# Fifth row tile of the early output projection: operand split before the barrier, products in the ramp behind it

## The reference

```python
h = rms_norm(x, g_attn); proj = h @ w_in          # 1376 columns for three groups of heads
out_a = sliding-window attention, 8 heads          # 512 columns
out_b = latent attention, 4 heads, chunk-causal    # 256 columns
out_m = cross-attention into 256 memory tokens     # 256 columns
x = x + concat(out_a, out_b, out_m) @ w_o          # 1024 x 1024
x = x + square(relu(rms_norm(x, g_ffn) @ w_ff1)) @ w_ff2
```

## Time and profile before

| what | value |
|---|---|
| time, median of 3 runs | 2163.74 us (2161.92 to 2166.23) |
| profiled execution, own time | 2162.71 us |
| its span | 2160.9 us |
| mean granted TensorE clock | 0.992 |
| busy, share of the span | PE 98%, PE weight loads 81%, DVE 67%, ACT 48%, POOL 51% |
| front and drain end (last PE matmul) | 437.6 us |
| first PE matmul behind the barrier | 440.5 us |
| first step of the second block (slot 24) | 500.9 us |

### The profile page before, as it was taken

One profiled execution on the slowest core, in us unless ns is written; L12 is line 12 of the kernel. 1 busy time (PEld: TensorE's weight loads), 2 busy tenths in 40 slices (PEclk: granted clock), 3 DMA queues, 4 the chain that ended last, 5 costly groups with the idle time before them and its releaser, 6 DMA issues. The chain is left out here.

```text
span 2160.9 us, 30875 instructions
## 1 busy us (share of the span) xinstructions
PE 2107.1 (98%) x9992; PEld 1744.5 (81%) x9992; DVE 1437.2 (67%) x2110; ACT 1039.3 (48%) x1870; POOL 1092.5 (51%) x892
## 2 busy tenths in 40 slices
PE   8999999899999999989999999999999999999999
PEld 6899999777777777768888878888888888888887
DVE  5788888977666656578777787766635644344463
ACT  6566666567767667644333443333423223222221
POOL 2566665635565767568656676556346710020220
PEclk9999999999999999999999999999999999999999
DMA  7133243688676666755444654444677762233363
GB/s 244 44 110 96 84 117 117 209 244 249 191 214 199 200 194 202 250 182 180 160 155 146 238 186 150 143 142 159 221 241 276 243 204 100 98 137 134 134 221 114
DMA packets 293440, 374.20 MB, mean 173 GB/s; under 512 B 27149, under 2 KB 187117, under 8 KB 291518
## 3 DMA queue, kind: packets, MB, share of 16 engines
q1 hardware_dynamic: 293310, 372.56, 53.6%
HBM read 247.28 MB, written 125.19 MB: 172 GB/s over the span
## 5 line engine op out<-in xcount | busy, mean ns | idle before, releaser
L128 PE MATMUL bank<-f_t_hi,f_w_hi 128*128 128x512 f32 x896 | 351.0, 392 | 12.5 <-DVE f_w_lo L1888 7.1
L128 PE MATMUL bank<-f_t_lo,f_w_hi 128*128 128x512 f32 x896 | 350.3, 391 | 0.0
L128 PE MATMUL bank<-f_t_hi,f_w_lo 128*128 128x512 f32 x896 | 350.2, 391 | 0.0
L128 PE MATMUL bank<-f_w_hi,f_a_hi 128*128 128x512 f32 x896 | 348.5, 389 | 0.0
L128 PE MATMUL bank<-f_w_lo,f_a_hi 128*128 128x512 f32 x896 | 348.5, 389 | 0.0
L128 PE MATMUL bank<-f_w_hi,f_a_lo 128*128 128x512 f32 x896 | 348.5, 389 | 0.0
L2732 POOL TENSOR_TENSOR a_p_lo<-a_prob,a_p_hi 128x512 fp32r<-128x512 f32 (+1 forms) x192 | 233.9, 1229 | 168.2 <-DVE a_p_hi L2881 69.0
L128 PEld LDWEIGHTS bank<-f_t_hi,f_w_hi 128*128 128x128 f32 x896 | 169.3, 189 | 50.9 <-issue 14.4
L2140 DVE TENSOR_TENSOR f_a_lo<-f_a_raw,f_a_hi 128x1024 fp32r<-128x1024 f32 x112 | 160.2, 1430 | 72.2 <-ACT f_a_hi L2064 71.9
L2039 POOL TENSOR_TENSOR f_r<-f_r,f_y 128x512 f32<-128x512 f32 x24 | 42.0, 1785 | 325.0 <-DMA f_r<-s_x 325.0
L128 PEld LDWEIGHTS bank<-f_t_hi,f_w_lo 128*128 128x128 f32 x896 | 169.2, 189 | 35.3
(11 more groups left out here) (347 smaller groups left out, 4834.8 us busy)
## 6 DMA issues: line engine op xcount, KB each, us to landing
f_a_raw<-s_aop SPq DMA_DIRECT2D x112, 512.0 KB, 4.5
w_raw<-in_w_ff SPq DMA_DIRECT2D x64, 512.0 KB, 5.3
s_aop<-f_a SPq DMA_DIRECT2D x128, 256.0 KB, 4.5
s_aop<-f_s SPq DMA_DIRECT2D x96, 256.0 KB, 2.4
f_w_raw<-in_w_ff SPq DMA_DIRECT2D x64, 256.0 KB, 5.6
f_t_raw<-s_hop SPq DMA_DIRECT2D x14, 1024.0 KB, 8.1
f_r<-in_w_ff SPq DMA_DIRECT2D x48, 256.0 KB, 6.1
a_vals<-s_v SPq DMA_DIRECT2D x40, 264.0 KB, 4.9
```

Source lines behind the costliest of these rows:

```text
L128: ins = pe.matmul(out, a, b, start=(first and j == 0), stop=(last and j == n - 1))
```

## The change

1. SP issues a fifth `load_swa` in the drain (row tile 4) between the first and the second early store. 2. ACT makes its high part right after that of row tile 3, DVE its low part just before `rotate_latents` of the last tile; both go to buffers of their own, the low part over the place of the first early store, for which DVE waits (a semaphore of its own, `first_stored`). 3. Behind the barrier row tile 4 needs no split and no semaphore on PE: its 8 portions stand in slots -6, -6, -5, -5, -4, -4, -3, -2, its second half in another bank (`banks[6]`). 4. Its two adds both stand in DVE's slot 0 (the expression reads `(half + later) if v else 0`). 5. Row tiles 5 to 7 spread over slots 0, 1, 4, 5 / 8, 9, 12, 13 / 16, 17, 20, 21. 6. SP loads row tile 5's operand at slot -15, in the place where that of row tile 4 was loaded, and its x at slot -9, ahead of the loads of later slots; row tile 5's split moves from slot 3 to slot -3 on ACT and from slot 5 to slot -1 on DVE. 7. The other edits renumber semaphore counts (row tile 4 no longer counts splits) and keep the first write into `mixed`, which lies over the new buffers, behind both halves.

```diff
+    next_hi, next_lo = at("next_hi", [P, HP, P], m_at + 8 * KB, F32R), at("next_lo", [P, HP, P], x_at, F32R)
...
-        sp.dma_start(S["x_local"][v * P:(v + 1) * P, :], x2[v][:, :]).then_inc(stored, 16)
+        sp.dma_start(S["x_local"][v * P:(v + 1) * P, :], x2[v][:, :]).then_inc(first_stored if v == 0 else stored, 16)
...
+    def split_next_hi(ac):
+        ac.wait_ge(swa_loaded[NE % 2], 16 * (NE // 2 + 1))
+        ac.activation(next_hi[:, :, :], swa[NE % 2][:, :, :], ACT.Copy).then_inc(next_hi_done, 1)
+
+    def split_next_lo(dve):
+        dve.wait_ge(next_hi_done, 1)
+        dve.wait_ge(first_stored, 16)
+        dve.tensor_tensor(next_lo[:, :, :], swa[NE % 2][:, :, :], next_hi[:, :, :].bitcast(F32), ALU.subtract)
...
     def all_stored(eng):
-        eng.wait_ge(stored, 16 * NE)
+        eng.wait_ge(first_stored, 16)
+        eng.wait_ge(stored, 16 * (NE - 1))
...
                     E["store"](sp, 0)
+                    E["load_swa"](sp, NE)
                     first_loads(sp, R, S, (3, 4))
...
                     E["split_m_hi"](ac, 3)
+                    E["split_next_hi"](ac)
                     exponent(tc)
...
                     latent_low(tb, 1, pD, l_hi, l_lo)
+                    E["split_next_lo"](dve)
                     rotate_latents(tc)
...
-    RAMP = -6
-    visits, portion_slot = [], []
-    LOCAL_OF = (range(NE, 8), range(8, 11), range(11, 13), range(13, NT), ())
+    visits, portion_slot = [(NE, 0)], [-6, -6, -5, -5, -4, -4, -3, -2]
+    LOCAL_OF = (range(NE + 1, 8), range(8, 11), range(11, 13), range(13, NT), ())
...
-        lo, n = first_slot[u] if u else RAMP, 2 * (len(local) + len(other))
+        lo, n = first_slot[u], 2 * (len(local) + len(other))
...
-        if part == 0:
-            put("swa_load", max(first - 9, split_slot[LOCAL[t - NE - 2]] + 1 if t >= NE + 2 else -1000), v)
+        if part == 0 and v:
+            put("swa_load", -15 if v == 1 else max(first - 9, split_slot[LOCAL[t - NE - 2]] + 1 if t >= NE + 2 else -1000), v)
...
-        put("added", half + later, (v, 0))
-        put("added", last + later, (v, 1))
+        put("added", half + later if v else 0, (v, 0))
+        put("added", last + later if v else 0, (v, 1))
...
-            return pY
+            return banks[6] if (v, a) == (0, 1) else pY
...
+                if U == 0:
+                    ac.wait_ge(y_made, 2)
...
-                b, part = m_of(v), visits[v][1]
+                part = visits[v][1]
+                mh, ml = (m_hi[m_of(v)], m_lo[m_of(v)]) if v else (E["next_hi"], E["next_lo"])
...
-                if k == 0 or k == 1 and v in EARLY:
+                if v and (k == 0 or k == 1 and v in EARLY):
                     pe.wait_ge(m_lo_done, split_count(v, k))
```

More of the change, by code:

```diff
@@ L256, in early_visits @@
     x_loaded, stored = [sem(f"x_loaded{v}") for v in range(NE)], ctx.enter_context(nc.semaphore("e_stored"))
+    first_stored, next_hi_done = ctx.enter_context(nc.semaphore("e_first_stored")), sem("next_hi_done")
     def m_split_wait(eng, v):
@@ L342, in early_visits @@
                 first_highs=first_highs, first_lows=first_lows,
+                next_hi=next_hi, next_lo=next_lo, split_next_hi=split_next_hi, split_next_lo=split_next_lo,
                 all_stored=all_stored, store_last=store_last, sems=sems, end=m_at)
@@ L2432, in split_count @@
         if v in EARLY:
-            return v + 1 if k in early(v) else v + 1 + len(EARLY)
-        return v + 1 + (len(EARLY) if v > EARLY[-1] else 0)
+            return v if k in early(v) else v + len(EARLY)
+        return v + (len(EARLY) if v > EARLY[-1] else 0)
     tail = portion_slot[(NV - QT) * 2 * KH]
@@ L2445, in attend_and_project @@
         split_slot[v] = first - 3
-        if part == 0:
-            put("swa_load", max(first - 9, split_slot[LOCAL[t - NE - 2]] + 1 if t >= NE + 2 else -1000), v)
+        if part == 0 and v:
+            put("swa_load", -15 if v == 1 else max(first - 9, split_slot[LOCAL[t - NE - 2]] + 1 if t >= NE + 2 else -1000), v)
         if v in EARLY:
             put("m_split", N + LAG - 1, (v, early(v)))
-        put("m_split", N + LAG + 1 if v in EARLY else tail + 8 if v == NV - 1 else first - 3, (v, tuple(k for k in range(KH) if k not in early(v))))
+        if v:
+            put("m_split", N + LAG + 1 if v in EARLY else tail + 8 if v == NV - 1 else first - 3, (v, tuple(k for k in range(KH) if k not in early(v))))
         later = 1 if v < NV - QT else 0
-        put("added", half + later, (v, 0))
-        put("added", last + later, (v, 1))
+        put("added", half + later if v else 0, (v, 0))
+        put("added", last + later if v else 0, (v, 1))
         last += later
@@ L2653, in sync @@
                 sp.wait_ge(R["front_mo_stored"][t % 2], 16 * (t // 2 + 1))
-                if t >= NE + 2:
-                    sp.wait_ge(m_lo_done, LOCAL[t - NE - 2] + 1)
+                if t > NE + 2:
+                    sp.wait_ge(m_lo_done, LOCAL[t - NE - 2])
                 sp.dma_start(swa[t % 2][:, :, :], S["mix"][:, :, t * P:(t + 1) * P]).then_inc(swa_loaded[t % 2], 16)
@@ L2825, in scalar @@
                         E["all_stored"](ac)
-                    ac.wait_ge(swa_loaded[t % 2], 16 * ((t - NE) // 2 + 1))
+                    ac.wait_ge(swa_loaded[t % 2], 16 * ((t - NE + 1) // 2))
                     ac.activation(m_hi[v % 2][:, :, :], swa[t % 2][:, :, :], ACT.Copy).then_inc(m_hi_done, 1)
@@ L2843, in scalar @@
             for j in of("w_split", s):
-                ac.wait_ge(m_lo_done, NV + len(EARLY))
+                ac.wait_ge(m_lo_done, NV + len(EARLY) - 1)
                 if j == P5:
@@ L3032, in tensor @@
                     pe.wait_ge(w_lo_done, k + 1)
-                ins = products(pe, y_bank(v, a)[:, :], [(m_hi[b][:, k, :], m_lo[b][:, k, :], high[:, k, cols_o], low[:, k, cols_o])],
+                ins = products(pe, y_bank(v, a)[:, :], [(mh[:, k, :], ml[:, k, :], high[:, k, cols_o], low[:, k, cols_o])],
                                first=(k == 0), last=(k == KH - 1))
```

4 lines of the change are left out of this document (2 added, 2 removed).

## The result

The changed kernel takes 2169.14 us (median of 11 runs, 2168.04 to 2174.78), the kernel before 2164.09 us in the same session (11 runs, 2161.84 to 2167.09): ratio 1.0024, 95% interval 1.0016 to 1.0032. It is slower, by some 5 us, and outside the range that was given (2158.9 to 2165.8). The profiled execution has a span of 2168.1 us and an own time of 2169.86 us. Ratios go by the fast runs, which leaves out one run of experiment 4 of 8056 us.

The account below looks back on a forecast made before the run. PE bounds the first block, yields to ACT and DVE around slot 24, then bounds again. 2.7 - 0.4 - 0.6 = 1.7 us off 2162.71 gives 2161.0, or 2162.0 on the median's footing; range 2158.9 to 2165.8.

Parts of the forecast that it names:

- Drain: Before the barrier: row tile 4's added load, high part and low part (0.65 us) fit idle time; cost 0.
- When does the clock rise?: Ramp behind the barrier: clock rises at about 444.2, 3.7 us after PE resumes at 440.54; step 0 at about 449.1.
- The prediction's other answer: Ramp: warming up goes by time under load, run-variable; with the rise only at 449.7, step 0 at about 451.3.
- would still cost nothing: Ramp: a clock rise only at 449.7, step 0 at about 451.3, costs nothing, as the wait there ends later.
- The new wait: Before row tile 5's first portion: PE idles some 1.7 us for early stores, split and add, until about 451.55.
- Rival C: Clock falls in PE's idle of some 1.7 us before row tile 5's first portion: 3.3 us price, 2165.3; chance 0.12.
- Where ACT and DVE take over: Around slot 24: ACT and DVE limit PE's gain; smallest slack taken, 1.7 us, bounds 0 and 4.4.
- 0.4 for portions that stand in pairs: First block: slots 2 and 3 hold no products, step 4 waits for step 2's exponents; about 0.4 us lost.
- rival B: Late load, or ACT and DVE tangled with PE running in bursts, takes the whole gain: 2163.7 us; chance 0.15.
- Rival A: Last early store lands before 448, no new wait, ACT and DVE slack enough: gain 4.4 us, 2159.3; chance 0.17.

Follow-up runs that it names:

- experiment 4: Changed kernel with row tiles 5 to 7 in their old slots, row tile 4 still in the ramp: 2167.92 us, ratio 1.0011 to the kernel before.
- experiment 6: Kernel before with only the change's drain part (products, splits and adds in their old slots): 2165.50 us against 2166.08, ratio 0.9998.
- experiment 3: Changed kernel with 14 additional matmuls on PE ahead of row tile 5's first portion, but behind its wait: 2172.54 us, ratio 1.0032 to the kernel before.
- third trace of the changed kernel: Changed kernel, nothing edited, profiled once more in the session of the late kernel of 12: 2169.47 us, one run.
- experiment 8: Changed kernel with row tile 3's turned-row stores moved behind the key loads, plus 16 matmuls ahead of PE's wait for row tile 5's add: 2162.26 us, ratio 0.9992.
- experiment 2: Changed kernel with the fourth early store issued as SP's first work behind the barrier: 2167.58 us, ratio 1.0009 to the kernel before.
- experiments 9: Changed kernel with the fourth early store first behind the barrier and row tile 3's turned-row stores behind the key loads: 2160.80 us, ratio 0.9980 to the kernel before.
- the three moves: Fourth early store first, row tile 3's turned-row stores late, row tile 8's split a slot earlier: changed kernel 2158.30 us; kernel before with the last two 2158.25.
- experiment 7: Row tile 3's turned-row stores moved behind the key loads, in both kernels: changed kernel 2164.01 us, ratio 0.9983; kernel before 2160.16 us, ratio 0.9970.
- the late kernel of 12: Kernel before with 18 additional matmuls ahead of row tile 8's first portion, behind its waits: 2169.75 us against 2166.61, ratio 1.0016.
- experiment 1: Changed kernel again, nothing edited: 2170.75 us against 2164.96 for the kernel before, ratio 1.0031.
- experiment 10: Changed kernel with the three moves: 2158.30 us, ratio 0.9971 to the kernel before.
- experiment 5: Kernel before, nothing edited, three more traces; no separate time is given, clock over 645 to 660 was 0.89, 0.89 and 0.77.

## Why the prediction was wrong

**Drain: right in the sum.** No cost, shown by 6. The low part was mis-sized (2.07 us for 0.65), longer than the idle of 1.48 us that was to hold it, and still the drain ends no later.

**"When does the clock rise?": wrong.** It took the clock of the earlier trace rows over into a stretch that was to be loaded differently. With chunks alone in the ramp the clock behind the resume was 0.50 to 0.52 in five of eight traces and 0.69 to 0.72 in three; with the products between them PE is busy at once, and it was 1.00 from the resume on in nine of ten (in experiment 3 it fell on the way). Only the third trace of the changed kernel started at half. So the products cost 0.23 us each and not 0.43, PE is at the wait sooner and gains nothing, since the store sets its end. The prediction's other answer, that the rise comes at a run-variable time by the Trainium skill, TensorE: Matmul & The Clock Gate, Part 1, fits the spread (step 0 at 6.88, 6.87 and 9.65 us in three traces of one kernel), but not the level that nearly all of them show. That a late rise "would still cost nothing" was wrong by the prediction's own numbers: step 0 at 451.3 and 0.7 us for it and chunk 9 put PE at 452.0, behind the 451.55 at which the wait was to end.

**The new wait: mechanism right, size wrong.** The chain was as forecast, its end at 11.34 us behind the resume (forecast 11.0), but the idle was 3.71 us and not 1.7, because PE came to it 1.6 us sooner (7.6 us behind the resume, forecast 9.3). In other executions the store landed 4.2 to 5.8 us behind its issue (3.0 at the head of the queue), and the hole was 3.5 to 5.0 us where the ramp ran at full clock and nothing was put in the hole.

**Rival C is what happened**, with the chance 0.12. Its bound, between 1.50 and 1.98 us of idle, was read from one execution and held nearly everywhere in the eighteen traces (last section); what was wrong is the hole, put at 1.7 us and so between the two lengths, and the price of 0 that the sum gave to the clock. Its price at this place was 1.3 us (experiment 8), not 3.3; but it was also paid at slot 24, where the prediction saw no danger: a wait grown from 1.50 to 2.12 us was followed by half clock in seven of the eight traces that have it (not in experiment 8).

**"Where ACT and DVE take over": the step that failed most.** It read two idle times of DVE and one of ACT and kept the smallest slack as gain, 1.7 us. With the store moved to the front this much does reach slot 24: it comes at 58.87 and 58.53 us there (experiments 2 and 9), against 60.35 to 60.77 in six traces of the kernel before and its edits. But it does not get past it. The forecast had DVE's low part for row tile 8 release PE 1.7 us sooner than the 63.2 us behind the resume of the earlier trace rows; in these two traces it did so 0.8 and 1.1 us sooner, and the clock fell behind the wait and took 1.6. At step 26 both are behind the kernel before (68.91 and 68.59 against 68.14 to 68.50 in five traces).

The longer wait is not PE being early: it is 2.11 to 2.14 us whether slot 24 comes at 58.53 or at 65.00 us, and 1.48 to 1.51 in the eight traces in which row tiles 5 to 7 keep their old slots and row tile 8's split its place (experiments 4 and 6 among them). So it comes with the new slots, which end at 21 and leave 22 and 23 without a portion. ACT's high part of w_o, on which DVE's two low parts hang, starts 0.26 us ahead of slot 24's row in the kernel before, and 0.54 and 0.55 us behind it in experiment 2 and in the third trace of the changed kernel. The prediction moved the portions and left this wait as it was.

The third trace has the ramp and the hole about as forecast, and slot 24 came not 1.7 us sooner but 0.4 later. Of these 2.1 us, 0.8 were there at the first portion (11.8 us behind the resume, forecast 11.0). Between the first portion and slot 24 the forecast had 46.7 us and allowed 1.0 on top (0.4 for portions that stand in pairs, 0.6 for the slack); the trace took 49.1, which is 2.4 on top: 1.4 is more idle of PE, most of it for DVE's maxima, and 1.0 was not traced.

With the three moves the gain left is 0 (2158.30 against 2158.25), which is rival B's outcome by DVE's order and the clock behind its wait, not by DMA.

Rival A had its first condition met in experiments 2 and 9, a landing before 448, and its 4.4 us did not come: a wait of 1.39 us stayed, at slot 24 PE led by 2.0 us (58.53 against 60.57, experiments 9 and 7), at step 26 by nothing. The 3.2 us that was estimated there for the landing was met at the head of the queue (3.0 to 3.1 us), not at its end.

**Step 81 was not in the prediction.** It cost 4.3 us between the first two traces, and part of that is the luck of the first: from step 28 to the mark the other three traces of before took 2.1 to 3.0 us more. What is left looks like a cost of the change: that stretch takes 194.07 to 195.74 us in all seven traces with the split in the drain and the queue as it was (waits of 3.71 to 5.07 us), 190.73 to 193.72 in all five without (2.89 to 3.84 us, the late kernel of 12 among them), 2.0 us apart in the means of the two kernels of the study. The ratios leave 2.4 to 3.9 us to this place (0.24 to 0.31% in all, 0.13% without it). Against it stands experiment 6, whose median shows no loss. Lateness is not the reason, by the trace of 12. What makes the wait longer stays open.

**The account.** By the traces the changed kernel loses 3.3 us up to step 28 (75.28 to 76.48 us against 72.62 to 72.98) and 2.0 from there to the mark; the medians differ by 5.05, and by 5.8 in experiment 1. Of the first part, the hole and the clock behind it are worth 3.2 us (2170.75 to 2167.58 as the store moves to the front, one session). What then remains at slot 24 is net 0.6 us by the medians of experiments 9 and 7 (2160.80 against 2160.16), 0.35 at step 26 by their traces and 2.2 by their ratios, all within the scatter between sessions. The gain forecast, 1.7, is 0.

In the prediction's terms: the new wait, put at some 1.7 us at full clock, was 3.71 us with 1.3 us of half clock behind it, and the gain of 1.7 at the place where ACT and DVE take over was a longer wait, 2.12 us for 1.50, with 1.6 us of half clock behind it.

## What to carry to other kernels

Work moved out of a stretch in which PE is busy 98% wins only what the engines behind PE can follow: go to the next place where another engine ends PE's wait, ask what that engine itself waits for, and whether the new order of work makes the wait longer. A wait that grows from 1.5 to 2.1 us costs 0.6 us of idle and, here, 1.6 us of clock. A transfer that is waited for should be issued first, not last, in its burst; moving one store to the head of the queue was worth 3 us (experiments 1 and 2), and moving a blocked store behind the loads queued after it 6 us (experiment 7), more than the change could have brought. Two traces of one kernel should be read before a clock level or the length of one wait is put into a sum.

## What the runs showed of the hardware

Behind none of PE's idles of 1.0 to 1.51 us, from row tile 5's first portion to step 81 in the eighteen traces, did the clock fall, save one of 1.41 us that followed another of 1.83 us closely (experiment 4). Behind those of 1.72 us (experiment 10), 1.95 us (3) and 2.11 to 2.14 us (seven traces of eight) it fell, and so it did behind 3.36 to 5.07 us. The length of an idle alone does not settle it: behind 2.12 us in experiment 8 and behind 2.89 us at step 81 in the first trace the clock stayed, behind 3.49 us there it fell after some 1.3 us at full speed, and behind 3.50 us, in another trace, it had fallen at once (durations of 0.48 and 0.76 us in experiment 5).

The barrier's 3 us were followed by the full clock where dense work came at once (nine traces of ten), and mostly by the half clock where single chunks came (0.50 to 0.52 over the ramp in five traces of eight). One fall cost 1.3 us behind the hole and 1.6 at slot 24.

A 512 KB store landed 3.0 to 3.1 us behind its issue at the head of SP's burst and 4.2 to 5.8 us behind it at the end.
